# Experts of a MoE block on one core: half of the down product from float32 to three rounded products

## The reference, cut to what matters

```python
D_MODEL = 1024; N_EXPERTS = 64; TOP_K = 2; D_EXPERT = 256
def expert_block(args):
    xb, e = args
    hb = jax.nn.silu(xb @ w_gate[e]) * (xb @ w_up[e])      # rows x 1024 @ 1024 x 256, twice
    return hb @ w_down[e]                                  # rows x 256 @ 256 x 1024
```

## Time and profile before

| | us |
|---|---|
| median of 3 runs | 3007.86 (3005.77 to 3012.45) |
| the profiled execution | 3009.71 |
| its span, first to last instruction | 3007.8 |
| busy in the span: TensorE | 2543.5 (85%) |
| VectorE | 1730.5 (58%) |
| ScalarE | 1145.1 (38%) |
| GpSimd | 509.1 (17%) |
| DMA, one queue of SP (q1), share of 16 engines | 41.5% |
| mean granted clock of TensorE | 0.933 of full speed |

### The profile page before, as it was taken

How to read it: one execution, slowest core, us unless ns; L and a number is a source line. 1 busy time by engine, 2 the same in 40 slices (tenths; PEclk the granted TensorE clock), 3 DMA queues, 4 the chain that set the end, 5 groups by cost and what they waited for, 6 DMA issues and landing times. The chain is left out here.

```text
span 3007.8 us, 40627 instructions
## 1 busy us (share of the span) xinstructions
PE 2543.5 (85%) x12335; PEld 2047.1 (68%) x12335; DVE 1730.5 (58%) x2408; ACT 1145.1 (38%) x1622; POOL 509.1 (17%) x465
## 2 busy tenths in 40 slices
PE   4999999999997598899939886997499999999750
PEld 3888889899985487788817665775366666666530
DVE  6576584967712487787845453444455555555425
ACT  4110111134412376677732222212355555656420
POOL 2122222211100011111103221011211111211110
PEclk9999999999998799999969997998699999999975
DMA  5121211213321533434058867554388889988739
GB/s 127 51 84 37 81 49 63 70 71 106 106 95 59 143 86 87 112 100 132 15 141 193 194 171 228 175 174 181 110 334 331 338 341 368 349 335 344 281 133 394
DMA packets 227934, 510.61 MB, mean 170 GB/s; under 512 B 30268, under 2 KB 150076, under 8 KB 189404
## 3 DMA queue, kind: packets, MB, share of 16 engines
q1 hardware_dynamic: 194738, 411.80, 41.5%
q10 hardware_dynamic: 10626, 55.14, 4.5%
q0 software_dynamic: 22448, 42.16, 4.2%
HBM read 413.28 MB, written 133.46 MB: 182 GB/s over the span
## 5 line engine op out<-in xcount | busy, mean ns | idle before, releaser
L91 PE MATMUL project_bank<-project_xnT_hi,project_w_hi 128*128 128x512 f32 (+4 forms) x1352 | 512.1, 379 | 0.8 <-DVE project_xnT_lo L593 0.7
L92 PE MATMUL project_bank<-project_xnT_lo,project_w_hi 128*128 128x512 f32 (+4 forms) x1352 | 499.9, 370 | 0.0
L93 PE MATMUL project_bank<-project_xnT_hi,project_w_lo 128*128 128x512 f32 (+4 forms) x1352 | 497.8, 368 | 0.0
L2284 DVE TENSOR_TENSOR experts_gu_lo<-weights_gate_up,experts_gu_hi 128x2048 fp32r<-128x2048 f32 x136 | 306.4, 2289 | 134.3 <-ACT experts_gu_hi L2210 133.8
L641 DVE SCALAR_TENSOR_TENSOR project_work<-project_work,project_taps 128x2048 f32<-128x2048 f32 x128 | 341.4, 2667 | 18.6 <-DVE project_work L637 0.6
L2210 ACT ACTIVATE experts_gu_hi<-weights_gate_up 128x2048 fp32r<-128x2048 f32 x136 | 259.2, 1911 | 96.5 <-DMA weights_gate_up<-in_w_up_dram 70.6
L91 PEld LDWEIGHTS project_bank<-project_xnT_hi,project_w_hi 128*128 128x128 f32 (+1 forms) x1352 | 252.5, 187 | 35.6 <-issue 6.7
L92 PEld LDWEIGHTS project_bank<-project_xnT_lo,project_w_hi 128*128 128x128 f32 (+1 forms) x1352 | 252.4, 187 | 32.9 <-issue 6.1
L93 PEld LDWEIGHTS project_bank<-project_xnT_hi,project_w_lo 128*128 128x128 f32 (+1 forms) x1352 | 252.6, 187 | 26.9
L1013 DVE TENSOR_TENSOR attend_pT<-attend_t_bank,attend_pT 128x512 fp32r<-128x512 f32 (+3 forms) x352 | 212.5, 615 | 86.2 <-ACT attend_pT L963 83.8
L2175 PE MATMUL experts_y_bank<-weights_down,experts_hT 128*128 128x512 f32 x544 | 248.8, 600 | 3.9 <-issue 3.3
(11 more groups left out here) (249 smaller groups left out, 4316.8 us busy)
## 6 DMA issues: line engine op xcount, KB each, us to landing
weights_gate_up<-in_w_gate_dram SPq DMA_DIRECT2D x68, 1024.0 KB
weights_gate_up<-in_w_up_dram SPq DMA_DIRECT2D x68, 1024.0 KB
weights_down<-in_w_down_dram SPq DMA_DIRECT2D x68, 1024.0 KB, 6.6
project_w_raw<-in_w_in_dram SPq DMA_DIRECT2D x36, 512.0 KB, 4.1
qk_d<-project_work SPq DMA_DIRECT2D x16, 1032.0 KB, 5.3
gate_d<-project_work ACTq DMA_DIRECT2D x16, 1024.0 KB, 3.9
merge_gates<-gate_d SPq DMA_DIRECT2D x64, 256.0 KB, 5.3
merged_d<-merge_m_pair SPq DMA_DIRECT2D x64, 256.0 KB, 4.1
```

What stands on the lines that cost most here:

```text
L91: pe.matmul(out, lhs[0], rhs[0], start=first, stop=False)
L92: pe.matmul(out, lhs[0], rhs[1], start=False, stop=False)
L93: return pe.matmul(out, lhs[1], rhs[0], start=False, stop=last)
L2284: nc.vector.tensor_tensor(gu_lo[:, b, :, cut, :], gu_raw[:, b, :, cut, :], raw(gu_hi[:, b, :, cut, :]), ALU.subtract).then_inc(gu_lo_ready, 1)
```

## The change

For jobs 0 to 62 down is replaced by down_right_split. The left 512 columns of the result stay a plain float32 product of hT and down_raw: 2 matmuls. The right 512 columns become rounded products: 2 chunks by 3, on hT_hi, hT_lo, down_hi and down_lo. These four are new tiles, double buffered, 1024 or 256 values a partition and buffer. ScalarE writes the rounded parts: high_down, out of down_raw, and high_hidden, out of the PSUM bank with the turned hidden rows. VectorE writes the rests: low_down and low_hidden. In ScalarE's step high_down stands between high_x and the first half of high_gate_up, high_hidden between that half and take_hidden. In VectorE's step low_down and low_hidden stand between lower_x and lower_gate_up. low_hidden waits for hT_hi_ready and for hT_ready, so for take_hidden too. The right half of the product waits for down_lo_ready and hT_lo_ready. Four semaphores are added. No load is added or moved in SP's order, and the further jobs keep the old down.

```diff
--- before.py
+++ after.py
@@ -1939,6 +1939,10 @@
         silu = sb("silu", [P, DE])
         hidden = sb("hidden", [P, 2, DE])
         hT = sb("hT", [P, 2, HC, P])
+        hT_hi = sb("hT_hi", [P, 2, HC, P], F32R)
+        hT_lo = sb("hT_lo", [P, 2, HC, P], F32R)
+        down_hi = sb("down_hi", [P, 2, HC, 512], F32R)
+        down_lo = sb("down_lo", [P, 2, HC, 512], F32R)
         y_sb = sb("y_sb", [P, 2, D])
         table = sb("table", [P, EXPERTS], I32)
         columns = sb("columns", [P, MORE_JOBS + 1], I32)
@@ -1969,6 +1973,10 @@
         hidden_ready = sem("hidden_ready")
         hidden_turned = sem("hidden_turned")
         hT_ready = sem("hT_ready")
+        hT_hi_ready = sem("hT_hi_ready")
+        hT_lo_ready = sem("hT_lo_ready")
+        down_hi_ready = sem("down_hi_ready")
+        down_lo_ready = sem("down_lo_ready")
         down_done = sem("down_done")
         y_ready = sem("y_ready")
         to_row_ready = sem("to_row_ready")
@@ -2165,6 +2173,20 @@
                     m = nc.tensor.transpose(gu_bank[:, b, c * P:(c + 1) * P], by_chunk[:, c, :], ident[:, :])
                 m.then_inc(hidden_turned, 1)
 
+            def down_right_split(n, b, q):
+                pe.wait_ge(down_loaded[b], q * 16 + 16)
+                pe.wait_ge(hT_ready, n + 1)
+                pe.wait_ge(y_ready, n + 1)
+                for c in range(HC):
+                    nc.tensor.matmul(y_bank[:, b, 0, :], hT[:, b, c, :], down_raw[:, b, c, 0:512],
+                                     start=c == 0, stop=c == HC - 1)
+                pe.wait_ge(down_lo_ready, n + 1)
+                pe.wait_ge(hT_lo_ready, n + 1)
+                for c in range(HC):
+                    m = pair_matmuls(nc.tensor, y_bank[:, b, 1, :], (hT_hi[:, b, c, :], hT_lo[:, b, c, :]),
+                                     (down_hi[:, b, c, :], down_lo[:, b, c, :]), c == 0, c == HC - 1)
+                m.then_inc(down_done, 1)
+
             def down(n, b, q):
                 pe.wait_ge(down_loaded[b], q * 16 + 16)
                 pe.wait_ge(hT_ready, n + 1)
@@ -2184,12 +2206,12 @@
                     turn_hidden(n - 1, 1 - b)
                 gate_up(n, b, 1)
                 if before >= 1:
-                    down(n - 1, 1 - b, q + (b - 1))
+                    down_right_split(n - 1, 1 - b, q + (b - 1))
 
             turn_rows(0, 0, 0)
             over_first_jobs(pe, step)
             turn_hidden(EXPERTS - 2, 0)
-            down(EXPERTS - 2, 0, EXPERTS // 2 - 1)
+            down_right_split(EXPERTS - 2, 0, EXPERTS // 2 - 1)
 
             def further_products(n, b, q):
                 gate_up(n, b, 0)
@@ -2227,6 +2249,18 @@
                 nc.scalar.activation(hT[:, b, :, :], gu_bank[:, b, 0:DE].rearrange("p (c t) -> p c t", t=P),
                                      ACT.Copy).then_inc(hT_ready, 1)
 
+            def high_down(n, b, q):
+                wait(act, down_loaded[b], q * 16 + 16)
+                wait(act, down_done, n + 1)
+                nc.scalar.activation(down_hi[:, b, :, :], down_raw[:, b, :, 512:1024], ACT.Copy)\
+                  .then_inc(down_hi_ready, 1)
+
+            def high_hidden(n, b):
+                wait(act, hidden_turned, n + 3)
+                wait(act, down_done, n + 1)
+                nc.scalar.activation(hT_hi[:, b, :, :], gu_bank[:, b, 0:DE].rearrange("p (c t) -> p c t", t=P),
+                                     ACT.Copy).then_inc(hT_hi_ready, 1)
+
             def take_y(n, b):
                 wait(act, down_done, n + 3)
                 wait(act, y_free, n + 1)
@@ -2240,8 +2274,12 @@
                     take_y(n - 2, b)
                 if after >= 1:
                     high_x(n + 1, 1 - b)
+                if before >= 1:
+                    high_down(n - 1, 1 - b, q + (b - 1))
+                if after >= 1:
                     high_gate_up(n + 1, 1 - b, q + b, 0)
                 if before >= 1:
+                    high_hidden(n - 1, 1 - b)
                     take_hidden(n - 1, 1 - b)
                 if after >= 1:
                     high_gate_up(n + 1, 1 - b, q + b, 1)
@@ -2253,6 +2291,8 @@
             over_first_jobs(act, step)
             gate(EXPERTS - 2, 0)
             take_y(EXPERTS - 3, 1)
+            high_down(EXPERTS - 2, 0, EXPERTS // 2 - 1)
+            high_hidden(EXPERTS - 2, 0)
             take_hidden(EXPERTS - 2, 0)
             take_y(EXPERTS - 2, 0)
 
@@ -2288,6 +2328,17 @@
                 wait(dve, x_hi_ready, n + 1)
                 nc.vector.tensor_tensor(xT_lo[:, b, :, :], x_bank[:, :, :].rearrange("p k (c t) -> p (k c) t", t=P),
                                         raw(xT_hi[:, b, :, :]), ALU.subtract).then_inc(x_lo_ready, 1)
+
+            def low_down(n, b):
+                wait(dve, down_hi_ready, n + 1)
+                nc.vector.tensor_tensor(down_lo[:, b, :, :], down_raw[:, b, :, 512:1024], raw(down_hi[:, b, :, :]),
+                                        ALU.subtract).then_inc(down_lo_ready, 1)
+
+            def low_hidden(n, b):
+                wait(dve, hT_hi_ready, n + 1)
+                wait(dve, hT_ready, n + 1)
+                nc.vector.tensor_tensor(hT_lo[:, b, :, :], gu_bank[:, b, 0:DE].rearrange("p (c t) -> p c t", t=P),
+                                        raw(hT_hi[:, b, :, :]), ALU.subtract).then_inc(hT_lo_ready, 1)
 
             def times_up(n, b):
                 wait(dve, silu_ready, n + 1)
@@ -2311,6 +2362,10 @@
                     take_list(n - 2, b, list_of(n - 2))
                 if after >= 1:
                     lower_x(n + 1, 1 - b)
+                if before >= 1:
+                    low_down(n - 1, 1 - b)
+                    low_hidden(n - 1, 1 - b)
+                if after >= 1:
                     lower_gate_up(n + 1, 1 - b, 0)
                     lower_gate_up(n + 1, 1 - b, 1)
 
@@ -2322,6 +2377,8 @@
             lower_x(0, 0)
             over_first_jobs(dve, step)
             times_up(EXPERTS - 2, 0)
+            low_down(EXPERTS - 2, 0)
+            low_hidden(EXPERTS - 2, 0)
             take_list(EXPERTS - 3, 1, list_of(EXPERTS - 3))
             take_list(EXPERTS - 2, 0, list_of(EXPERTS - 2))
 
```

## The result

The changed kernel takes 3025.07 us (median of 7 runs, 3013.89 to 3032.81), the kernel before 3008.5 us in the same measurement (7 runs, 3000.86 to 3012.45). The ratio is 1.0056, with a 95% interval of 1.0042 to 1.0069: 17 us slower. A second measurement on another occasion gave 1.0049 (1.0031 to 1.0067). The forecast of no change was wrong. The range, 2992 to 3028, held because it was drawn out to the slower rival, and the time is that rival's, 3025.

The account below looks back on a forecast made before the run. The flow of weight loads was taken to pace the jobs. Start -1 us, 58 load-paced jobs 0, end +0.8: together -0.2, so no change and 3008 us, range 2992 to 3028.

Parts of the forecast that it names:

- forecast of no change: Whole kernel: weight loads pace the jobs, so the time stays 3008 us, range 3002 to 3014; chance 0.42.
- slower rival: Gather takes a fixed time from its issue: +0.27 us a job, 3025 us, 3028 with high_down uncovered; chance 0.25.
- The bound: First jobs: the flow of weight loads paces them at 10.7 us, with TensorE's own 10.08 us just under it.
- 341 GB/s is the job's 10.7 us itself: DMA loads of the first jobs: 3.66 MB a job at that rate was said to fill the job's time.
- term of 0.09: TensorE's down product: the first rounded product behind another kind takes 0.32 us, not 0.23, adding 0.09 a job.
- the cover: ScalarE: high_down, 1.02 us, fits the idle wait for gate and up weights, mean 1.0, so costs nothing on the path.
- I take 0: GpSimd's gather, issued 0.8 us later, was priced at no cost, with 0.8 kept for the range.
- Two pairs of rows: Two jobs' gathers, landing 11.52 and 8.33 us from issue, taken as evidence that landing is tied to the loads.
- point of decision: Gather: the fixed-time case holds if it takes over 9 us even when issued 1.8 us or more behind its load.
- forecast's signs: Between 2200 and 2800 us: jobs of 10.7 us, TensorE's row wait about 0.65, ScalarE's weight wait near 0 a job.
- faster rival: Loads issued on TensorE's cue: at least half its saving comes through, -8 us to 3000, all 2992; chance 0.25.
- last rival: TensorE's new block waits for hT_lo or down_lo, or switching costs more than 0.09: 3009 to 3033; chance 0.08.

Follow-up runs that it names:

- e2: The kernel before, with the index of the gather written about 6 us earlier, behind the subtract of the turned rows: 0.9944, -17 us.
- e5: The changed kernel with the index of the gather written about 6 us earlier, behind the subtract of the turned rows: 0.9934 of the kernel before, 2988 us.
- e7: The changed kernel with high_down behind gate and low_down behind the list of the scatter: 1.001 of the kernel before.
- e6: The changed kernel with low_hidden between the two gate and up subtracts instead of ahead of both: 0.9993 of the kernel before.
- e10: The changed kernel with low_hidden between the gate and up subtracts and high_down behind gate, gather where it was: 0.9998 of the kernel before.
- e1: The kernel before, with an idle VectorE subtract of about 0.8 us ahead of each index, so the gather alone goes later: 1.0035, +10.5 us.
- e4: The changed kernel with the right half as plain float32 again, all four splits still done and waited for: 1.006 of the kernel before, +18 us.
- e9: The changed kernel as it is, measured again on another occasion: 1.0049 of the kernel before.
- e3: The changed kernel without the four splits, rounded products on tiles written once, right 512 columns not the product: 0.9965 of the kernel before, -10.5 us.

## Why the prediction was right or wrong, point by point

**The bound.** Wrong in its weight. The weights were late in 49 of 56 jobs, but late for ScalarE, which had slack behind them; the rows were late for TensorE in half of the jobs, and that was the path. e2 shows it: with the rows early, the weights become nearly twice as late and the kernel 17 us faster. The reading "341 GB/s is the job's 10.7 us itself" was circular: bytes over time gives the rate whatever sets the time. The DMA engines can move 351 GB/s here, and with the rows early they are what is late next, at 10.3 us a job (e2, e5); that is close to the prediction's estimate of 10.2 us, worked out from the limit of 358 GB/s in the Trainium skill ("DMA: Bandwidth & Descriptors", section Specifications).

**TensorE.** The saving was 0.34 us a job, not 0.25: the term of 0.09 for the switch of kinds was not there between the two halves of the down product (3.10 us in all). The unhindered job went from 10.08 to 9.74.

**ScalarE.** The added durations were right, the cover was not. The mean idle time of 1.0 us was just the length of high_down, and in the mean the rounding of gate and up did not start later (3.3 us after the turn, 3.4 before). But 10 of 55 jobs before started it 2.2 to 2.7 us after the turn, and after the change none starts before 3.1. The prediction priced such jobs at 3.5 us in all, and only in the slower rival. e7 gives back 12 us and more by moving high_down, with low_down behind it. That those jobs were the ones in which the kernel caught up is an argument, and e6 and e10 speak against it as the whole story: in e6 too no rounding starts before 3.1 us, in e10 18 of 56 start within 2.7 us, and the two are equally fast.

**VectorE.** Right: +0.88 us for the pair of subtracts against +0.8, through low_hidden's wait for hT. The issue of loads moved as said: the down load from 10.6 to 10.3 us after the turn, the gate load still 0.9 behind it.

**The later gather.** This is the step that failed: "I take 0". Alone, the idle subtract of 0.8 us cost 10.5 us (e1), and the splits, which move the gather by the same 0.8 us, cost 18 (e4). Two pairs of rows stood for a tie of the landing to the loads. Over the nine kernels with the gather in its old place, in the 335 jobs in which TensorE waited for rows, the picture is (means, us):

| gather behind down load | jobs | load to landing | gather to landing |
|---|---|---|---|
| under 0.5 | 16 | 10.5 | 10.2 |
| 0.5 to 1 | 39 | 10.9 | 10.2 |
| 1 to 1.5 | 119 | 11.0 | 9.8 |
| 1.5 to 2 | 128 | 11.3 | 9.6 |
| 2 and more | 33 | 11.9 | 9.7 |

Neither end is fixed. Counted from the loads, a gather issued 1 us later lands roughly 0.6 us later. The landing shows only in jobs where TensorE waited, so this is a comparison of late jobs with late jobs. The two pairs differed by far more than that, 8.33 and 11.52 us, for other reasons (one of them belongs to the longest job of the stretch, 12.7 us from turn to turn). The rule of the Trainium skill that a DMA engine serves its queues in turn ("DMA: Bandwidth & Descriptors", section Queues, rings and completion order), set aside in the prediction, gave the right sign: the landing does move with the gather's own issue, if not in full (0.6 us for 1 us). No run shows how the DMA engines shared their time. What keeps a gather of 0.25 MB for 9.6 us and more, no run here shows.

**The rivals.** The slower one gave 3025, and 3025.07 was measured. Its direction and its path, the later gather, are the right ones; that the number fits so well is luck, two errors that cancel. It took 25 us for the later gather, where e1 measured 10.5 and all the splits together 18 (e4), and it subtracted 8 us for TensorE's saving, which was lost. Its point of decision, gathers of over 9 us from issue at 1.8 us behind the load, is what the timelines show. Its other signs came only in part: turns of rows 10.8 us apart in the mean and 0.73 us of wait for rows a job in the profiled execution, 10.9 and 0.8 in e9's, where it asked for 10.9 to 11.0 and over 1. The forecast's signs, 10.7 us, 0.65 and near 0 for ScalarE's wait, were about as near: shares and waits alone don't tell the two apart. The faster rival's half of the saving is real in e3, -10.5 us where -8 was written. The last rival, a wait inside the new block, did not occur.

## What to carry to other kernels

A mean idle time that an added operation just fills is not proof of cover: look at how many repeats have less of it, and test it by moving the operation. Where a late transfer's request stands at the end of an in-order stream, an operation put ahead of it is paid, here in part, by whoever waits for the transfer, even if both engines have idle time. Move the request first (here one line, worth 17 to 20 us against the kernel before), then the change can be judged by itself. Bytes over time give the rate whatever sets the time: a rate says nothing about the bound until a run has moved something else and left the bytes alone, as e2 does.

## What the runs showed of the hardware that was not expected

- A plain float32 block of 4 records followed by 6 rounded products of 512 columns takes 3.10 us (2491.80 to 2494.67 and one spacing of 0.23), with no loss at the change of kind; two records of plain float32 are 0.86 us and three rounded products 0.69.
- A gather of 0.25 MB (28.75 MB over 57 gathers and 56 scatters between 2200 and 2800 us before, the mean of both) lands 9.6 to 10.2 us after its issue, in the jobs that waited for it, while the core's DMA moves 332 to 346 GB/s in all. The time from issue shrinks by some 0.6 us when it is issued 1.5 us later behind the loads. With the gather issued 6.5 us earlier (e2) the same 16 DMA engines move 351 GB/s instead of 341.
